# A gated linear recurrence on one Trainium2 core: both directions of a chunk share score products and one score matrix, and the backward state runs at the end

## The chip, the cores and the metric

The kernel runs on one core of one Trainium2 chip (trn2). The metric is the device time of one execution in microseconds (us). The engines are named as the profile names them: PE (matmuls), PEld (its weight loads), DVE, ACT, POOL and SP. SP and POOL issue most of the transfers here; their queues appear as SPq and POOLq.

## The reference, cut to what matters

One layer of a backbone: an input projection, two mixing branches (a 2-D Fourier transform over 2048 positions and the channels of four groups, and a gated linear recurrence run forwards and backwards), a merge, an output projection and an MLP. The change touches only the recurrence and the Fourier work that is interleaved with it. All of it is float32. Per direction and head (4 heads, 128 x 128 state):

```python
# S_t = diag(f_t) S_{t-1} + k_t v_t^T,   o_t = S_t^T q_t,   k = 1 - f
f = lb + (1.0 - lb) * sigmoid(f_pre)
scores = einsum('bhtk,bhsk,bhtsk->bhts', qc, kc, decay)   # inside a chunk, masked
o = o_inter(qc * exp(b), S) + einsum('bhts,bhsv->bhtv', scores, vc)
S_new = exp(b_last) * S + einsum('bhsk,bhsv->bhkv', kc * exp(b_last - b), vc)
o = o_f + o_b[:, :, ::-1]      # both directions are added
```

256 context tokens come first, and their final state starts the 2048 latent tokens, in each direction.

## The kernel before, in words

`phase_mix` (L600 to L1094) is one stage of the program. A **unit** is one chunk of 128 tokens in one direction: 4 context units, then 32 latent units, forward and backward alternating (`run`, L699). Forward units walk up from token 0, backward ones down from token 2047.

**Decays by levels.** The running products of the gates inside a chunk are built as a tree of 7 levels (block sizes B = 1 to 64, `LEVELS`). `gates` (L749) does per level two DVE multiplies of 128 x 512: the decayed operands for the score product (L755, `mix_lev`), then the tree step in place (L759, `mix_w`), which waits for L755. `mix_lev` holds for each position either its key or its query, by which half of its block of 2B it is in, so a product (L919) takes all 128 columns as weights and only the 64 query columns as the moving operand. There is one such product per level and head; a diagonal product with undecayed keys (L925) is separate. Every float32 matmul shows as two matmul instructions.

**Masking.** `mask_score` (L784) copies each score block under a mask into the unit's score matrix `pm` (L793, 128 x 256, six times; L798, 128 x 512, the diagonal); ACT copies level 64 (L1013). DVE interleaves the masking of unit k with the gates of unit k+1.

**State and output.** `whole` (L763) multiplies keys and queries by the whole-chunk decays (L769, 128 x 1024). PE transposes the keys (L856), ACT copies them (L959), PE forms the state's addition (L862), DVE makes the new state with four small instructions (L778). `output` (L896) takes 16 matmul instructions (L902, L903), ACT copies the result (L986) and POOL stores it (L1035).

**The rest of a unit.** In the first 16 latent units PE also does one Fourier unit of the first pass (two products of 128 x 512, L870), in the last 16 one of the second pass (L876 twice, L883). ACT makes keys 1 - f (L950), POOL writes ones (L1026). SP loads gates, queries and values of a unit once its predecessor's state is new (`slot`, L723: wait, then L732, L733, L734). All engines run hardware loops over 4 units (`Fori`).

Of the kernel before, what the change touches and what calls it, by code (L numbers as in the profile page):

```python
# [20 lines left out]
I32 = mybir.dt.int32  # L21
# [578 lines left out]
def phase_mix(nc, d, g):  # L600
# [3 lines left out]

    NU, NX, HP, W2 = 2 * NTT, TC // P, H * P, 2 * H * P
    SL = 4
    X = 2 * NX
    with Box(nc, "mix") as bx:
        w = bx.sb("w", [P, 2, 2, 2, HP])
        qk = bx.sb("qk", [P, 2, 2, 2, HP])
        v = bx.sb("v", [P, 2, 2, BR])  # L630
        lev = bx.sb("lev", [P, 2, NL, HP])
        qkd = bx.sb("qkd", [P, 2, 2, HP])
        pm = bx.sb("pm", [P, 2, HP])
        kdT = bx.sb("kdT", [P, 2, HP])
        st = bx.sb("st", [P, 2, HP])
        ost = bx.sb("ost", [P, 2, HP])
        mask = bx.sb("mask", [P, 2, NL - 1, 256], I32)
        diag = bx.sb("diag", [P, HP], I32)
        m1 = bx.sb("m1", [P, 2, 2, P])
        u_in = bx.sb("u_in", [P, 2, BR])  # L640
        a_st = bx.sb("a_st", [P, 2, 2, BR])
        m2 = bx.sb("m2", [P, 2, 2 * P])
        m3 = bx.sb("m3", [P, 2, P])
        xin = bx.sb("xin", [P, 2, 2, SL, P])
        zT = bx.sb("zT", [P, 2, 2, 512])
        fst = bx.sb("fst", [P, T])
        bank = bx.banks()
        SC, DG, TO, SS, FT = bank[0:4], bank[4], bank[5], bank[6], bank[7]
        ld_m = bx.sem("ld_m")
        ld = [[bx.sem(f"ld_{x}{s}") for s in range(2)] for x in "fb"]  # L650
        ld_n = [bx.sem(f"ld_n{i}") for i in range(2)]
        st_o, st_a = ([bx.sem(f"st_{n}{i}") for i in range(2)] for n in ("o", "a"))
        st_f = bx.sem("st_f")
        ld_x = [bx.sem(f"st_x{i}") for i in range(2)]
        step_s, ready, kk_done, ones, scores, masked, m64, trans, trcopy, o_mm, o_out, s_mm, s_new, f_mm, f_out = (
            bx.sem(n) for n in ("step", "lev_ready", "kk_done", "ones", "scores", "masked", "m64", "trans", "trcopy",
                                "o_mm", "o_out", "s_mm", "s_new", "f_mm", "f_out"))
        block = bx.block()
        ad = d["dft_a"]

        F2 = 2 * 16 - 12 * 4

        def at(i, k, per, c):

            return i * (SL * per) + (k * per + c)

        def halves(ap, B):
            return ap.rearrange("p (m two b) -> p m two b", two=2, b=B)  # L670

        def key_half(dr):
            return dr

        def halves_of(buf, dr, s, B):

            t = buf[:, dr, s]
# [18 lines left out]
        def pre_of(dr, s):  # L696
            return w[:, dr, s, 1 - key_half(dr)]
# [1181 lines left out]
```

## Time and profile before

| | us |
|---|---|
| median of 3 runs | 3809.98 (3809.21 to 3812.9) |
| span of the profiled execution | 3805.7 |
| what lies around that span, against the median | 4.3 |
| `phase_mix`, first load issued to last store issued | 1190.9 to 1757.4 |
| PE busy, share of the span | 3434.8 (90%) |
| DVE busy, share of the span | 1994.6 (52%) |

The profiled execution has no separate device time beside its span, so the span is compared with the median. The share of busy time is over the whole program; the stage that changes is one seventh of it and has its own limits. In the timeline an entry gives start, duration, engine, line, operation and count; a count above 1 merges neighbours, so the spacing of starts tells more than the durations, which overlap. PEclk is the granted TensorE clock: 1.00 is 2.4 GHz, 0.50 is 1.2 GHz.

### The profile page before, as it was taken

How to read it: one execution, taken by the hardware profiler on the slowest of the kernel's cores; microseconds unless marked ns; L12 is line 12 of the kernel's file. 1: busy time of each engine (PE TensorE's matmuls, PEld its weight loads, DVE VectorE, ACT ScalarE, POOL GpSimd, SP SyncE). 2: the span in 40 equal slices, each digit the busy share in tenths (PEclk: the TensorE clock that was granted, in tenths of full speed). 3: DMA queues.
4: the chain of work that ended last, by engine and by line, in shares of the span. 5: the costliest groups of instructions: out<-in, count | busy, mean ns of one | idle time of the engine just before them, and what ended most of it. 6: DMA issues, size and time to landing. Idle time of an engine off the chain costs nothing. (4 is left out here: it accounts for less than half of the span.)

```text
span 3805.7 us, 42879 instructions
## 1 busy us (share of the span) xinstructions
PE 3434.8 (90%) x16080; PEld 2863.9 (75%) x16080; DVE 1994.6 (52%) x2898; ACT 498.3 (13%) x825; POOL 211.1 (6%) x318
## 2 busy tenths in 40 slices
PE   6879999999896899996796968999999689999997
PEld 6867777777785788884575757888888478888885
DVE  3730000000124998995786658555555585555556
ACT  1211111111000122222100002111111021111110
POOL 0011100000000111110000000000000000000000
PEclk9699999999997788998898989999999899999998
DMA  6831122221213344342654342111111221111111
GB/s 209 279 119 66 66 66 77 72 66 56 77 64 104 102 124 123 111 122 105 194 168 151 134 161 72 44 44 44 50 44 50 86 86 58 47 44 44 49 50 45
DMA packets 257179, 349.40 MB, mean 92 GB/s; under 512 B 13107, under 2 KB 189507, under 8 KB 252358
## 3 DMA queue, kind: packets, MB, share of 16 engines
q1 hardware_dynamic: 225078, 221.86, 19.2%
q0 software_dynamic: 26208, 108.55, 8.2%
q10 hardware_dynamic: 5808, 17.83, 1.4%
q8 instruction: 56, 0.92, 0.1%
q14 instruction: 29, 0.24, 0.0%
HBM read 250.14 MB, written 98.05 MB: 91 GB/s over the span
## 5 line engine op out<-in xcount | busy, mean ns | idle before, releaser
L137 PE MATMUL mlp_bank<-mlp_h2h,mlp_w1h 128*128 128x512 f32 x1024 | 406.8, 397 | 23.0 <-ACT mlp_a L1670 23.0
L137 PE MATMUL proj_bank<-act_hTh,proj_wh 128*128 128x512 f32 x1024 | 401.8, 392 | 18.6 <-PE proj_bank L139 17.5
L1637 DVE TENSOR_TENSOR mlp_acc<-mlp_acc,mlp_bank 128x512 f32<-128x512 f32 x480 | 321.8, 685 | 175.6 <-PE mlp_bank L139 175.6
L137 PE MATMUL mlp_bank<-mlp_w2h,mlp_ah 128*128 128x512 f32 x1024 | 402.5, 393 | 9.8 <-DVE mlp_acc L1590 9.8
L139 PE MATMUL mlp_bank<-mlp_h2h,mlp_w1l 128*128 128x512 f32 x1024 | 406.0, 396 | 0.0
L138 PE MATMUL mlp_bank<-mlp_h2l,mlp_w1h 128*128 128x512 f32 x1024 | 405.9, 396 | 0.0
L139 PE MATMUL mlp_bank<-mlp_w2h,mlp_al 128*128 128x512 f32 x1024 | 401.1, 392 | 0.0
L138 PE MATMUL mlp_bank<-mlp_w2l,mlp_ah 128*128 128x512 f32 x1024 | 400.8, 391 | 0.0
L138 PE MATMUL proj_bank<-act_hTl,proj_wh 128*128 128x512 f32 x1024 | 398.6, 389 | 0.0
L139 PE MATMUL proj_bank<-act_hTh,proj_wl 128*128 128x512 f32 x1024 | 398.5, 389 | 0.0
L427 DVE CAST proj_wh<-proj_raw 128x1024 fp32r<-128x1024 f32 x40 | 27.8, 695 | 640.2 <-PEq L454 634.8
L919 PEld LDWEIGHTS mix_bank<-mix_lev 128*128 128x128 f32 x1792 | 238.7, 219 | 30.8 <-issue 22.6
L1628 DVE CAST mlp_ah<-mlp_a 128x512 fp32r<-128x512 f32 x128 | 54.9, 429 | 389.4 <-ACT mlp_a L1688 389.3
L919 PE MATMUL mix_bank<-mix_lev 128*128 128x64 f32 x1792 | 239.8, 302 | 21.1 <-DVE mix_pm L798 21.1
L137 PEld LDWEIGHTS mlp_bank<-mlp_h2h,mlp_w1h 128*128 128x128 f32 x1024 | 193.0, 189 | 70.4 <-ACT mlp_a L1670 23.5
L137 PEld LDWEIGHTS proj_bank<-act_hTh,proj_wh 128*128 128x128 f32 x1024 | 192.1, 188 | 70.6 <-issue 30.5
L1686 ACT ACTIVATE mlp_a<-mlp_bank,mlp_b 128x512 f32<-128x512 f32 x128 | 88.3, 689 | 1161.6 <-PE mlp_bank L139 1145.0
L137 PEld LDWEIGHTS mlp_bank<-mlp_w2h,mlp_ah 128*128 128x128 f32 x1024 | 193.6, 189 | 53.6 <-DVE mlp_acc L1590 13.3
L139 PEld LDWEIGHTS mlp_bank<-mlp_h2h,mlp_w1l 128*128 128x128 f32 x1024 | 192.9, 188 | 47.4
L138 PEld LDWEIGHTS mlp_bank<-mlp_h2l,mlp_w1h 128*128 128x128 f32 x1024 | 193.1, 189 | 47.0
L139 PEld LDWEIGHTS mlp_bank<-mlp_w2h,mlp_al 128*128 128x128 f32 x1024 | 193.7, 189 | 41.3
L138 PEld LDWEIGHTS mlp_bank<-mlp_w2l,mlp_ah 128*128 128x128 f32 x1024 | 193.7, 189 | 40.6
(204 smaller groups left out, 5204.2 us busy)
## 6 DMA issues: line engine op xcount, KB each, us to landing
mlp_raw<-in_w SPq DMA_DIRECT2D x128, 512.0 KB, 4.0
scratch_proj<-proj_stage POOLq DMA_DIRECT2D x32, 1024.0 KB, 5.3
front_w<-in_w_ada SPq DMA_DIRECT2D x24, 1024.0 KB, 5.6
proj_raw<-in_w_in SPq DMA_DIRECT2D x40, 512.0 KB, 5.8
merge_gates<-scratch_proj SPq DMA_DIRECT2D x32, 512.0 KB, 5.1
front_x<-in_x ACTq DMA_DIRECT2D x8, 1024.0 KB, 6.1
scratch_xn<-front_x POOLq DMA_DIRECT2D x8, 1024.0 KB, 6.4
mix_w<-scratch_proj SPq DMA_DIRECT2D x32, 256.0 KB, 3.1
```

The source lines that it names most:

```text
L137: nc.tensor.matmul(out, wh, xh, start=(k == 0), stop=False)
L138: nc.tensor.matmul(out, wh, xl, start=False, stop=False)
L139: last = nc.tensor.matmul(out, wl, xh, start=False, stop=(k == k_tiles - 1))
L427: nc.vector.tensor_copy(wh[:, s], raw[:, s]).then_inc(w_hi, 1)
L919: last = nc.tensor.matmul(SC[li // 2][:, (li % 2) * 256 + h * 64:(li % 2) * 256 + h * 64 + 64], lv, halves(lv, B)[:, :, 1 - key_half(dr)], ...
L1628: nc.vector.tensor_copy(ah[:, z, cs], a[:, c, :]).then_inc(ahi_s, 1)
L1637: nc.vector.tensor_tensor(dst, dst, V[n % 4][:], ALU.add).then_inc(acc_s, 1)
L1686: nc.scalar.activation(a[:, c, :], U[2 * e + c][:], ACT.Relu, bias=bias).then_inc(relu_s, 1)
```

## The change

The stage is rewritten. A **chunk** now holds both directions: 2 context chunks, then 16 latent ones, walked forwards, all unrolled.

1. DVE per level: one multiply of 128 x 1024 makes keys and queries for both directions (`level`), and two tree steps of 128 x 512 (`tree`). The operand `kq` is a ring of 5 levels, and `level` waits for its own completion.
2. PE per level: one product of 128 x 128 per head fills the score blocks of both directions. Level 64 is made of two 64-wide products per head. The diagonal product takes the sum of both directions' keys, which POOL adds (`key_sum`).
3. One score matrix per chunk: six masked copies of 128 x 512 on DVE, levels 32 and 64 by six small ACT copies (`big`).
4. The forward output of a chunk already holds the scores of both directions. The backward state needs the chunks from the last to the first, so the decayed backward queries (`qd`), the additions (`ub`) and the totals (`tot`) of all chunks are kept, and after the last chunk 16 steps of `back_state`, `back_output` and a store follow.
5. Fourier units: 8 of the first pass ahead of everything, 2 a chunk in chunks 0 to 3, one of the second pass a chunk in chunks 4 to 15, the last 4 in the tail. Fourier products have two banks (`FT`).
6. A chunk needs 5 loads: two gates, the queries twice, the values.

The diff, cut to its core (of the removed lines only the loops stand here; the functions that they called are printed above):

```diff
-            for k in range(SL):
-                slot(0, k, 1)
-            with eng.Fori(1, 4) as i:
...
         @block.sync
+            def load_f(n):
+                b = n % 2
+                if n >= 2:
+                    sp.wait_ge(kd_s, n - 1)
+                    sp.wait_ge(tot_s, n - 1)
...
+                for row, dr in ((3, 0), (1, 1)):
+                    sp.dma_start(dec[:, b, row].rearrange("p (h t) -> p h t", h=H),
+                                 src[dr * BR:(dr + 1) * BR, cols].rearrange("(h p) t -> p h t", p=P)).then_inc(ld_f[b], 16)
+            def load_q(n):
+                b, c = n % 2, n - NX
+                if c >= 2:
+                    sp.wait_ge(qd_s, c - 1)
+                    sp.wait_ge(sc_s, 8 * (c - 2) + 1)
+                for row in (1, 3):
...
+            def load_u(j):
+                if j >= 2:
+                    sp.wait_ge(f_mm, 2 * (j - 2) + 2)
...
+            for n in range(NX):
+                load_f(n)
+                load_v(n)
+            sp.dma_start(mask[:], d["masks"]).then_inc(ld_m, 16)
+            load_q(NX)
+            for j in range(2):
+                load_u(j)
...
+            for j in range(2, 8):
+                load_u(j)
+            load_f(NX)
+            load_f(NX + 1)
+            for c in range(NC):
...
+                if c + 1 < NC:
+                    load_v(n + 1)
+                if c + 2 < NC:
+                    load_q(n + 2)
+                    load_f(n + 2)
         @block.vector
+            def tree(n, li):
+                B = LEVELS[li]
+                out, total = forward(n % 2, B)
+                step.up(nc.vector.tensor_tensor(out, out, total, ALU.mult))
+                out, total = backward(n % 2, B)
+                step.up(nc.vector.tensor_tensor(out, out, total, ALU.mult))
+            def level(c, li):
...
+                nc.vector.tensor_tensor(kq[:, r % NK, :], selected(qk[:, b].rearrange("p a t -> p (a t)"), LEVELS[li]),
+                                        selected(decays(b), LEVELS[li]), ALU.mult).then_inc(lev_s, 1)
+                dve.wait_ge(lev_s, r + 1)
...
+            def new_state(n):
+                dve.wait_ge(u_mm, 2 * n + 1)
...
+            for c in range(NC):
+                n = c + NX
+                loaded(n)
+                dve.wait_ge(ld_q[n % 2], 32 * ((c // 2) + 1))
+                for li in range(NL):
+                    level(c, li)
+                    tree(n, li)
+                    if li == 1:
+                        new_state(n - 1)
+                    if li == 2 and c == 0:
+                        dve.wait_ge(ub_s, 2)
+                        back_state(0, ub[:, NC - 1], tot[:, 0, 1], ub[:, NC - 2])
+                    if li < 6:
+                        score(c, li)
+                    step.wait(dve)
+                keys(n)
+                queries(c)
+            new_state(NU - 1)
+            for x in range(1, NC):
+                c = NC - x
+                if x >= 2:
+                    dve.wait_ge(o_mm, NC + x - 1)
+                dve.wait_ge(ub_s, NX + c + 1)
+                back_state(x, sb_[:, (x + 1) % 2], tot[:, NX + c, 1], ub[:, c])
         @block.tensor
+            for j in range(8):
+                for piece in range(2):
+                    fourier("a", j, piece)
+            transposes(0, 0)
+            transposes(0, 1)
...
+                diagonal(c)
+                level(c, 0)
+                transposes(n - 1, 0)
+                fourier(*parts[0])
+                level(c, 1)
+                transposes(n - 1, 1)
+                products(n - 1, 0)
+                level(c, 2)
+                fourier(*parts[1])
+                products(n - 1, 1)
+                level(c, 3)
+                if c:
+                    output(c - 1)
+                level(c, 4)
+                fourier(*parts[2])
+                level(c, 5)
+                if len(parts) > 3:
+                    fourier(*parts[3])
+                level(c, 6)
...
+            for x in range(NC):
+                back_output(x)
+                if x < len(rest):
+                    fourier("b", *rest[x])
         @block.scalar
...
+                key_copy(n - 1, 0)
+                fourier(*parts[0])
+                key_copy(n - 1, 1)
+                fourier(*parts[1])
+                back_copy(n - 1)
+                if c:
+                    output(c - 1)
+                fourier(*parts[2])
+                if len(parts) > 3:
+                    fourier(*parts[3])
+                big(c)
+                totals(n)
+                if c + 2 < NC:
+                    keys(n + 2)
...
         @block.gpsimd
+            def key_sum(c):
+                n = c + NX
+                pool.wait_ge(kk, n + 1)
...
+                nc.gpsimd.tensor_tensor(ks[:, c % 2], qk[:, n % 2, 0], qk[:, n % 2, 2], ALU.add).then_inc(ksum, 1)
```

In the last excerpt `keys` on ACT waits for both gate loads of its chunk, makes the two sets of keys and counts `kk`; `totals` copies the last decay columns once DVE has counted `kd_s` in `keys`; `products` on PE waits for the ACT copy of the transposed keys.

## Rows read from the trace of the kernel before

**Rows 1.** The page: span and instructions.

```profile
span 3805.7 us, 42879 instructions
```

**Rows 2.** Busy time by stretch: stretch, length, PE, PEld, DVE, ACT, POOL (count), PEclk, DMA, GB/s.

```profile
1242.00:1500.00 258.00, 233.84 (x1493) 208.55 (x1492) 236.33 (x413) 52.44 (x95) 40.65 (x67) 0.82 0.41 120
1500.00:1740.00 240.00, 235.23 (x1658) 210.29 (x1657) 219.66 (x387) 57.90 (x134) 40.48 (x60) 0.99 0.35 106
```

**Rows 3.** Timeline of DVE: one unit, and the first and last L769 of the loop.

```profile
1236.16 1.23 DVE L769 TENSOR_TENSOR mix_qkd<-mix_qk,mix_w 128x1024 f32<-128x1024 f32 x1
...
1577.81 1.22 DVE L769 TENSOR_TENSOR mix_qkd<-mix_qk,mix_w 128x1024 f32<-128x1024 f32 x1
1579.03 0.84 DVE L755 TENSOR_TENSOR mix_lev<-mix_qk,mix_w 128x512 f32<-128x512 f32 x1
1579.91 1.11 DVE L759 TENSOR_TENSOR mix_w<-mix_w 128x512 f32<-128x512 f32 x1
1581.05 0.69 DVE L755 TENSOR_TENSOR mix_lev<-mix_qk,mix_w 128x512 f32<-128x512 f32 x1
...
1589.27 0.68 DVE L759 TENSOR_TENSOR mix_w<-mix_w 128x512 f32<-128x512 f32 x1
1589.87 0.73 DVE L798 COPY_PREDICATED mix_pm<-mix_diag,mix_bank 128x512 f32<-128x512 int32 x1
1590.49 0.68 DVE L755 TENSOR_TENSOR mix_lev<-mix_qk,mix_w 128x512 f32<-128x512 f32 x1
...
1592.03 1.12 DVE L778 SCALAR_TENSOR_TENSOR mix_st<-mix_st,mix_w,mix_bank 128x128 f32<-128x128 f32 x4
...
1737.30 1.22 DVE L769 TENSOR_TENSOR mix_qkd<-mix_qk,mix_w 128x1024 f32<-128x1024 f32 x1
```

**Rows 4.** Timeline of PE: the first two at clock 0.50, the others at 1.00.

```profile
1240.31 1.91 PE L870 MATMUL mix_bank<-mix_u_in,mix_m 128*128 128x512 f32 x2
...
1261.93 2.02 PE L925 MATMUL mix_bank<-mix_qk 128*128 128x128 f32 x8
...
1737.70 6.36 PE L919 MATMUL mix_bank<-mix_lev 128*128 128x64 f32 x56
...
1743.90 1.11 PE L925 MATMUL mix_bank<-mix_qk 128*128 128x128 f32 x8
...
1744.85 1.89 PE L876 MATMUL mix_bank<-mix_m,mix_xin 128*128 128x256 f32 x8
```

**Rows 5.** Busy time by stretch where the clock falls and comes back.

```profile
1315.00:1316.00 1.00, 0.22 (x2) 0.23 (x3) 1.00 (x3) 0.32 (x2) 1.00 (x2) 1.00 0.82 249
1318.00:1331.00 13.00, 13.00 (x55) 11.63 (x55) 12.83 (x22) 0.74 (x2) 0.00 (x0) 0.50 0.21 62
1331.00:1332.00 1.00, 1.00 (x4) 0.41 (x4) 0.96 (x2) 0.44 (x1) 0.00 (x0) 0.89 0.00 0
```

**Rows 6.** Timeline of SP: a unit's first two load issues.

```profile
1561.36 0.37 SPq L732 DMA_DIRECT2D mix_w<-scratch_proj  x1
...
1561.91 0.40 SPq L733 DMA_DIRECT2D mix_qk<-scratch_proj  x1
```

**Rows 7.** Issue to landing of the third load (L734), 1240 to 1490 us.

```profile
DMA to landing us min/median/max: 3.3/3.8/6.4
```

**Rows 8.** Timeline of ACT: two sets of keys, one copy of a bank.

```profile
1224.63 1.34 ACT L950 ACTIVATE mix_qk<-mix_w,all_one 128x512 f32<-128x512 f32 x2
...
1755.75 0.59 ACT L986 COPY mix_ost<-mix_bank 128x512 f32<-128x512 f32 x1 [1.20 <-PE mix_bank L903]
```

**Rows 9.** Busy time by stretch, columns as in Rows 2: the stage's first loads.

```profile
1190.00:1200.00 10.00, 0.00 (x0) 0.00 (x0) 5.22 (x7) 0.72 (x1) 3.40 (x7) 0.50 0.71 148
1200.00:1210.00 10.00, 4.30 (x16) 3.21 (x16) 9.66 (x17) 2.69 (x5) 0.17 (x1) 0.50 0.74 285
```

**Rows 10.** Transfers of the stage, size and median us to landing.

```profile
scratch_o<-mix_ost POOLq DMA_DIRECT2D x30, 256.0 KB, 3.2
```

**Rows 11.** Timeline of POOL: the stage's last store.

```profile
1756.63 0.75 POOL L1035 DMA_DIRECT2D scratch_o<-mix_ost  x1 [1.23 <-ACT mix_ost L986]
```

More of the change, by code:

```diff
@@ L653, in phase_mix @@
+        st_o, st_a, ld_x = ([bx.sem(f"st_{x}{s}") for s in range(2)] for x in "oax")
         st_f = bx.sem("st_f")
[L654 to L657, printed above, removed]
+        step_s, kk, ones, ksum, lev_s, sc_s, masked, big_s, kd_s, qd_s, tot_s = (bx.sem(x) for x in (
+            "step", "keys", "ones", "key_sum", "level", "scores", "masked", "big", "keys_decayed", "queries_decayed", "totals"))
@@ L658, in phase_mix @@
+        trans, trcopy, u_mm, ub_s, new_s, o_mm, o_out, b_new, f_mm, f_out = (bx.sem(x) for x in (
+            "trans", "trcopy", "u_mm", "u_back", "state", "o_mm", "o_out", "state_back", "f_mm", "f_out"))
         block = bx.block()
         ad = d["dft_a"]
[L663 to L673, printed above, removed]
@@ new lines, in back_output @@
+            def back_output(x):
+                c = NC - 1 - x
+                pe.wait_ge(b_new, x + 1)
+                pe.wait_ge(o_out, NC + x)
+                for h in range(H):
+                    s = slice(h * P, (h + 1) * P)
+                    last = nc.tensor.matmul(OUT[:, s], sb_[:, x % 2, s], qd[:, c, s], start=True, stop=True)
+                last.then_inc(o_mm, 1)
+            for j in range(8):
+                for piece in range(2):
+                    fourier("a", j, piece)
@@ L947, in _ @@
+            transposes(NU - 1, 0)
+            transposes(NU - 1, 1)
+            fourier("b", 12, 0)
+            products(NU - 1, 0)
+            output(NC - 1)
+            fourier("b", 12, 1)
+            products(NU - 1, 1)
+            rest = [(j, piece) for j in range(12, 16) for piece in range(3)][2:]
+            for x in range(NC):
+                back_output(x)
+                if x < len(rest):
+                    fourier("b", *rest[x])
         @block.scalar
         def _(act):
-            def one_minus_f(dr, s):
-                nc.scalar.activation(qk[:, dr, s, key_half(dr)], pre_of(dr, s), ACT.Identity, scale=-1.0, bias=g["one"][:, 0:1]
-                                     ).then_inc(kk_done, 1)
@@ L1023, in _ @@
+            key_copy(NU - 1, 0)
+            key_copy(NU - 1, 1)
+            fourier("b", 12, 0)
+            output(NC - 1)
+            fourier("b", 12, 1)
+            back_copy(NU - 1)
+            rest = [(j, piece) for j in range(12, 16) for piece in range(3)][2:]
+            for x in range(NC):
+                output(NC + x)
+                if x < len(rest):
+                    fourier("b", *rest[x])
         @block.gpsimd
         def _(pool):
-            def suf_ones(dr, s):
-                nc.gpsimd.memset(w[:, dr, s, key_half(dr)], 1.0).then_inc(ones, 1)
```

708 lines of the change are left out of this document (345 added, 363 removed).

## The prediction, written before the changed kernel ran

> **What bounds the kernel now.** I read the page first: one execution spans 3805.7 us [rows 1], and only `phase_mix`, 1190.9 to 1757.4, is changed. Next the stretches of that stage: with the first-pass Fourier units PE is busy for 233.8 of 258 us and DVE for 236.3, at a mean granted clock of 0.82; with the second pass PE for 235.2 of 240 and DVE for 219.7, at 0.99 [rows 2]. Both engines are nearly full, so a cut on one alone buys only its lead over the other. Then DVE's timeline: from the first to the last L769 of the loop it is 501.1 us for 31 units, 16.2 us each [rows 3]; a unit on DVE, summed below by the same prices, is 15.1 us, so the remaining 1.1 us is DVE waiting for PE.
>
> **DVE, a chunk of both directions** [rows 3]. Spacing of starts counts, not duration. A multiply of 128 x 512 takes 0.60 us when the next instruction does not wait for it (1589.27 to 1589.87), its 0.69 plus 0.035 when it does; at B = 1 it takes 0.84 (L755) or 1.11 (L759). A multiply of 128 x 1024 takes 1.22. A masked copy of 128 x 512 takes 0.62 (1589.87 to 1590.49), the state 1.12. Hence:
> - levels 1 to 5: 1.255 (`level`, waited for) + 2 x 0.60 (`tree`) + 0.62 (`score`) = 3.08 each, 15.4;
> - level 0: 1.55 (1.255 plus twice the 0.15 that B = 1 adds to 0.69) + 2 x 1.02 + 0.62 = 4.2;
> - level 6, without a score: 1.255 + 0.60 + 0.725 = 2.6;
> - new state 1.12, keys 1.13, queries 1.22: 3.5.
>
> Sum 25.7 us a chunk, against 32.3 us measured for two units. That alone would give 16 x 6.6 = 106 us. Most of it goes again, at three places.
>
> **PE, a chunk.** At full clock 56 products of 64 columns take 6.36 us, 0.114 each, and 8 of 128 columns take 1.11 with their end, 0.111 from start to start [rows 4]. A 64-column product costs what a 128-column one does, so a level for both directions costs what one direction did: 0.9 us. Diagonal 0.9, six levels 5.4, level 64 (16 short products) 0.9 to 1.8, two sets of transposes (4 instructions each, half the group) 1.2, two of products 1.8, output 1.8, Fourier 3.4 (first pass, the low-clock 1.91 of L870 halved, four times) or 5.1 (L876 twice, and L883 like it): 16 to 17.5 us of 25.7. PE is no longer the bound at full clock; at half clock it needs 32 to 35.
>
> **First loss: a chain through four queues, every chunk.** Let E be the end of `queries`. SP waits for it, then issues four loads (queries twice, gates twice) about 0.5 apart [rows 6]; before, the first went out 0.17 after the state. The third load of a unit, issued 1.1 after the first, lands 3.8 later, 3.3 at the least [rows 7]; the fourth I put 0.9 behind it (an estimate: the issue distance of 0.55 and a little more transfer), so the gates are there at E + 5.85. ACT has `keys(n+2)` ahead of the `key_copy` of the next chunk: 1.34 for two sets, 0.59 for the copy [rows 8], done at E + 7.9. Only then can PE run the second set of transposes and the products (0.6 + 1.05): E + 9.65. DVE reaches `new_state`, which needs them, after level 0, level 1 and its tree: E + 4.2 + 2.46 = E + 6.7. It waits 3.0 us at full clock. At half clock these PE steps double: 4.3, and 5.8 if the level and the second-pass Fourier product ahead of them are at half clock too. By the least landing and full clock it is 2.4. In the last chunk, which follows no such loads, PE's order alone costs 1.4. I take 3.6, near the full-clock end because PE has wide products here: a chunk of 29.3 us, bounds 28.1 and 31.5. Behind the waiting `new_state` stand all further levels; PE idles for 3 us there, so nothing catches up.
>
> **Second loss: the head.** The first load goes out at 1190.9, and ahead of the first Fourier input stand 2.8 MB. By 1200 the queues had moved 1.5 MB, in the next 10 us 2.9 MB [rows 9]: it is there at about 1204. Eight Fourier units follow on PE before any key is transposed. Each must store two halves before its buffer is free: a store of that size lands after 3.2 [rows 10], plus copies and two issues 5.4 us for two units, so 2.7 each, to 1227. DVE's context work, 2 x 11.4 us, ends by 1220 and hides there. The gates of chunk 0 wait on SP for `totals(0)`, which is on ACT behind the eight units; loads, keys: DVE starts chunk 0 at 1233. It waits there for its two states (4 to 8 us, the first ones at low clock) and adds one `back_state`: chunk 0 takes 33, to 1266.
>
> **Third loss: the tail.** After the last chunk PE does transposes, two Fourier pieces, products and one output: the first `back_output` starts 9.5 us later (8.2 at full clock). Ten steps are a `back_output` of 0.9 and a Fourier piece of 1.73: 26.3. The last six are bound by the copy and store loop, 0.59 + 3.2 and hand-overs for two steps, 2 us, or 2.7 at low clock: 15.7 with the last store. 51.5 in all, bounds 50 and 56; before, the loop's last L769 was followed by 19 us to the end of the last store [rows 3, 11].
>
> **The sum.** 1266 + 14 x 29.3 + 27.5 (last chunk) + 51.5 = 1755.2, against 1757.4: 2 us shorter, a span of 3803.5. The median of the runs stands 4.3 above the span, so 3808 us. What follows the stage is unchanged. What the hardware loops cost per pass before is inside the 16.2; the unrolled chunks have no such term.
>
> **POOL's addition** (`key_sum`, 128 x 512) has no row; the nearest is POOL busy for 40.65 us with 67 entries [rows 2], 0.6 each. It starts when the keys are made, E + 7.3, while DVE waits for PE anyway. Beside DVE work it can cost nothing or hold DVE up for its own length; I take nothing, because it falls into the wait.
>
> **The clock.** After about 1.4 us in which PE had nothing to do (busy for 0.22 of the us from 1315, and for a part of the one before it) it ran from 1318 to 1331 at 0.50, the 1.2 GHz level, though busy all the time and mostly with 64-column products, and came back to 2.4 GHz in 1331 to 1332, behind 128- and 512-column ones [rows 5]. The new chunk leaves PE without work for about 3 us at two places, ahead of level 0 and behind `new_state`'s products, so stretches at half clock follow; I expect a mean of 0.65 to 0.8 in this stage, and have put 0.6 us for it into the wait of 3.6.
>
> **Rivals.**
> - *The chain is short.* The loads land like the fastest ones, PE is at full clock when the key copies come: 28.1 a chunk, 17 us less, and the head and tail at their short ends, another 5: 3786. For it: the least landing of 3.3, and no other queue is transferring at E. Against it: four loads instead of three. With the wait at its floor of 1.4, which only an order without the keys ahead of the copy would allow, 3772.
> - *Half clock decides.* Place: level 0, the Fourier piece and the transposes ahead of `new_state`. PE comes into each chunk after 3 us without work, so at 0.50: a wait of 5.8, 31.5 a chunk, +31, and 5 more in chunk 0 and the tail: 3844. It ends slower from a chunk of 30.0 on. For it: 0.82 already where PE was busy 9 tenths of the time [rows 2]. Against it: these products are twice as wide as those that ran for 13 us at 0.50 [rows 4, 5].
> - *POOL and DVE block each other.* If the chain is short, `key_sum` no longer falls into DVE's wait but beside its multiplies; with 0.6 us lost in each of 14 chunks on top of the forecast, 3816. It weighs most against the short chain. The Trainium skill, SBUF — State Buffer (section Who interferes with whom) has the rule for it: a DVE instruction with two SBUF inputs and a GpSimd instruction that reads SBUF contend, and the loser stands still. Before, POOL only wrote (its memsets), so no row bears on it; chance 0.03.
> - *The diff does not do what it says.* If each direction still had its own masked copies and its own products, DVE would stay at 16 us a direction; the diff speaks against it; 0.02.
>
> **The numbers.** A measurement of this kernel can tell 0.2%, 7.6 us, from no change. My forecast (waits near 3.6) has 0.36, the short chain 0.31, half clock 0.28, POOL 0.03, the diff 0.02. An error of 0.5 us in a chunk is already 8 us, so the middle case keeps 0.30 within 0.2%, and its rest is split between the sides: faster 0.36, slower 0.34. The forecast's own range is 3797 to 3819. Both large rivals belong in 8 of 10, short of the outermost floor: 3776 to 3847.
>
> **What would show it.** DVE without waits 25.7 a chunk; `new_state` waiting for PE's products 3 to 4.5 us in chunks 1 to 14 and 1.4 in the last; ACT's keys starting near E + 6; DVE's first `level` at 1233; 16 backward steps in about 41 us; PE busy for about 75% of the stage. Wrong would be: DVE waiting at the scores (PE late all over), a unit price of 128 x 1024 above 1.22, or a head that is much shorter because the Fourier units are not bound by their stores.

## The result, and the profile of the changed kernel

The median is 3817.62 us in 14 runs (3811.38 to 3825.12), beside 3809.60 for the kernel before in 14 runs on the same chip: a ratio of 1.0023, 95% interval [1.0015, 1.0031]. The change makes the kernel slower by 8 us (5.7 to 11.8). I had forecast 3808, a gain of 2: the time is inside the range of 3776 to 3847, but it moved the other way.

The profiled execution took 3825.12 us, the longest of the 14 and 7.5 above their median. The page and the busy time by stretch (columns as in [rows 2]); the recurrence runs from 1198.6 to 1778.6:

```profile
span 3823.4 us, 39338 instructions
PE 3322.9 (87%) x15056; PEld 2737.5 (72%) x15056; DVE 1936.6 (51%) x2650; ACT 532.7 (14%) x943; POOL 228.8 (6%) x313
```

```profile
1198.60:1244.00 45.40, 22.49 (x56) 9.80 (x56) 22.91 (x35) 14.74 (x28) 11.58 (x20) 0.76 0.83 254
1244.00:1377.00 133.00, 83.11 (x473) 65.44 (x474) 105.55 (x138) 32.01 (x74) 22.33 (x30) 0.82 0.32 98
1377.00:1700.00 323.00, 225.13 (x1452) 193.28 (x1452) 276.29 (x363) 82.70 (x209) 52.03 (x60) 0.89 0.27 82
1700.00:1740.00 40.00, 32.95 (x201) 28.75 (x202) 27.84 (x45) 11.10 (x27) 5.28 (x8) 0.87 0.17 56
1740.00:1778.60 38.60, 32.39 (x172) 26.67 (x171) 14.82 (x52) 14.43 (x30) 13.85 (x19) 0.87 0.41 126
```

What to see: the stage lasts 580.0 us against 566.4 before (1190.9 to 1757.4), +13.6. What stands ahead of it is the same code and took 7.7 us longer in this execution; in the twelve kernels below it took 1188.7 to 1197.3, so that is scatter. What follows took 3.5 less. So the span moved by 17.7 and the median by only 8; differences of a stage to these 580.0 can come out some us too large. PE was busy for 91 and 98% of the stretches of [rows 2]; now it has work for 62% of the second stretch and 70% of the third. DVE, at 79 to 86%, no longer fills its time either: neither engine's own work sets the length, so a wait between them does.

The chain of waits between engines names it. Columns: engine, its line, whom it waited for; us in total, times, the longest:

```profile
ACT mix_qk L1001 <- DMA mix_dec<-scratch_proj: 108.3, 16, 9.7
...
DVE mix_st L792 <- PE mix_bank L891: 72.6, 17, 7.2
...
PE mix_bank L858 <- DMA mix_fx<-in_dft_m: 38.6, 9, 19.3
...
DVE mix_kd L763 <- PE mix_bank L878: 14.0, 1, 14.0
```

The second line is the wait of `new_state` that the forecast is built on. It isn't the same in all chunks. From one L769 to the next, chunks 1 to 5 take 32.75, 32.01, 32.71, 32.11 and 31.83 us with waits of 7.24, 6.51, 7.20, 6.61 and 6.33; chunks 6 to 14 take 28.4 to 29.5 (28.9 on average) with 2.9 to 4.0; chunk 15 takes 27.62 with 2.11. Here is a late chunk (chunk 2) on the timeline (columns: start, us, engine, line, operation, count, idle time before and what ended it):

```profile
1311.67 0.99 SPq L687 DMA_DIRECT2D mix_dec<-scratch_proj  x2
1312.70 0.50 SPq L710 DMA_DIRECT2D mix_fx<-scratch_u  x1
1314.20 0.44 SPq L711 DMA_DIRECT2D mix_fx<-in_dft_m  x1
...
1317.68 0.72 ACT L1001 ACTIVATE mix_qk<-mix_dec,all_one 128x512 f32<-128x512 f32 x1 [7.88 <-DMA mix_dec<-scratch_proj]
1318.84 2.04 PE L858 MATMUL mix_bank<-mix_fx 128*128 128x512 f32 x2 [3.88 <-DMA mix_fx<-in_dft_m]
...
1322.07 0.60 PE L878 MATMUL mix_bank<-all_ident,mix_kd 128*128 128x128 f32 x4
1322.51 1.06 PE L891 MATMUL mix_bank<-mix_v,mix_kdT 128*128 128x128 f32 x8
1323.60 1.12 DVE L792 SCALAR_TENSOR_TENSOR mix_st<-mix_st,mix_tot,mix_bank 128x128 f32<-128x128 f32 x4 [6.51 <-PE mix_bank L891]
```

SP issues its loads in the order of the program. Its four loads for the chunk after next wait for L769 (end 1310.60 here), and **behind them stand the Fourier inputs of the chunk that has just begun**, issued from 1312.70 on. PE has a Fourier piece ahead of level 1, of the second transposes and of the products that the state needs. So it stands still for 3.88 us until the input has landed, and DVE behind it. And a steady chunk (11, the longest of the nine), with E, the end of L769, at 1582.71:

```profile
1583.76 1.00 SPq L687 DMA_DIRECT2D mix_dec<-scratch_proj  x2
...
1586.51 2.61 PE L864 MATMUL mix_bank<-mix_m,mix_fx 128*128 128x256 f32 x8
...
1589.60 0.72 ACT L1001 ACTIVATE mix_qk<-mix_dec,all_one 128x512 f32<-128x512 f32 x1 [7.69 <-DMA mix_dec<-scratch_proj]
1590.96 0.59 ACT L1015 COPY mix_kdT<-mix_bank 128x512 f32<-128x512 f32 x1
1591.60 0.66 PE L878 MATMUL mix_bank<-all_ident,mix_kd 128*128 128x128 f32 x4 [1.58 <-ACT mix_kdT L1015]
1592.09 1.06 PE L891 MATMUL mix_bank<-mix_v,mix_kdT 128*128 128x128 f32 x8
1593.19 1.12 DVE L792 SCALAR_TENSOR_TENSOR mix_st<-mix_st,mix_tot,mix_bank 128x128 f32<-128x128 f32 x4 [4.00 <-PE mix_bank L891]
```

That is the forecast's chain link by link: gates issued, landed, ACT's keys, the key copy behind them, transposes, products. It holds in all nine steady chunks: ACT's keys start 5.8 to 6.9 us after E (6.2 on average), and the wait is that time less 2.9 in eight of them, less 2.7 in chunk 12. The head and the tail:

```profile
1237.40 0.30 ACT L1008 COPY mix_tot<-mix_dec 128x4 f32<-128x4 f32 x2
...
1239.01 1.23 DVE L763 TENSOR_TENSOR mix_kd<-mix_qk,mix_dec 128x1024 f32<-128x1024 f32 x1 [13.98 <-PE mix_bank L878]
...
1242.28 0.72 ACT L1001 ACTIVATE mix_qk<-mix_dec,all_one 128x512 f32<-128x512 f32 x1 [2.75 <-DMA mix_dec<-scratch_proj]
...
1243.69 1.26 POOL L1110 TENSOR_TENSOR mix_ks<-mix_qk 128x512 f32<-128x512 f32 x1 [3.86 <-ACT mix_qk L1002]
1243.91 2.43 DVE L755 TENSOR_TENSOR mix_kq<-mix_qk,mix_dec 128x1024 f32<-128x1024 f32 x1 [2.88 <-ACT mix_qk L1002]
...
1738.92 1.05 PE L948 MATMUL mix_bank<-mix_qd,mix_stb 128*128 128x128 f32 x8
1741.54 1.05 PE L948 MATMUL mix_bank<-mix_qd,mix_stb 128*128 128x128 f32 x8
...
1771.56 2.05 PE L948 MATMUL mix_bank<-mix_qd,mix_stb 128*128 128x128 f32 x8 [0.77 <-ACT mix_ost L1034]
1774.37 2.05 PE L948 MATMUL mix_bank<-mix_qd,mix_stb 128*128 128x128 f32 x8 [0.77 <-ACT mix_ost L1034]
```

DVE's second set of context keys waits 14 us for transposes that PE does behind all eight Fourier units. The first chunk's multiply (L755) comes 45.3 us after the stage's start; it waits another 2.88 us for ACT's keys, whose gates SP issues at 1237.79, behind the totals that ACT copies at 1237.40, after its sixteen Fourier copies. In the tail a backward step with a Fourier piece takes 2.62; without one 1.9, and 2.8 at the low clock.

### The profile page after: what moved, and what is told of

Same layout as the page of the kernel before. It is cut to its first block and busy times, and to the rows that moved or that the text cites. A ratio compares the mean times of both kernels' runs of the same rounds, so it can differ in the third digit from the quotient of the medians.

```text
span 3823.4 us, 39338 instructions
## 1 busy us (share of the span) xinstructions
PE 3322.9 (87%) x15056; PEld 2737.5 (72%) x15056; DVE 1936.6 (51%) x2650; ACT 532.7 (14%) x943; POOL 228.8 (6%) x313
## 5 line engine op out<-in xcount | busy, mean ns | idle before, releaser
L427 DVE CAST proj_wh<-proj_raw 128x1024 fp32r<-128x1024 f32 x40 | 27.8, 695 | 640.3 <-PEq L454 635.0
L139 PEld LDWEIGHTS proj_bank<-act_hTh,proj_wl 128*128 128x128 f32 x1024 | 192.2, 188 | 40.2
L138 PEld LDWEIGHTS proj_bank<-act_hTl,proj_wh 128*128 128x128 f32 x1024 | 192.3, 188 | 38.8
```

Of the source, the lines that this page charges most:

```text
L138: nc.tensor.matmul(out, wh, xl, start=False, stop=False)
L139: last = nc.tensor.matmul(out, wl, xh, start=False, stop=(k == k_tiles - 1))
L427: nc.vector.tensor_copy(wh[:, s], raw[:, s]).then_inc(w_hi, 1)
```

## The experiments

Each kernel was run beside the kernel before. "Stage" is the length of the recurrence in the profiled execution (566.4 before, 580.0 after); the ratio is to the kernel before, with its 95% interval. The kernels stand in the order of the questions. The ratio is not the quotient of the two medians, so the two columns can differ by a few us; most in e3, whose ten times lie in two groups, four at 3796 to 3802 and six at 3814 to 3818 (the profiled one among them).

| kernel | ratio | median, difference to before | stage |
|---|---|---|---|
| e1_u_first | 1.0010 [0.9998, 1.0022] | +5 | 570.2 |
| e2_gates_first | 1.0006 [0.9994, 1.0018] | +3 | 564.1 |
| e3_keys_behind | 1.0004 [0.9987, 1.0021] | +9 | 576.6 |
| e5_sum_beside_mult | 1.0058 [1.0041, 1.0075] | +21 | 584.1 |
| e4_u_and_gates | 0.9966 [0.9956, 0.9977] | -15 | 550.5 |
| e6_ug_sum_at_state | 0.9968 [0.9956, 0.9980] | -13 | 552.9 |
| e7_head | 1.0040 [1.0025, 1.0055] | +19 | 581.5 |
| e8_all | 0.9961 [0.9947, 0.9976] | -13 | 552.6 |
| e9_piece_behind | 1.0050 [1.0031, 1.0069] | +16 | 577.7 |
| e10_keys_between | 0.9969 [0.9958, 0.9981] | -13 | 552.9 |
| e11_piece_too | 0.9965 [0.9951, 0.9978] | -14 | 538.2 |
| e12_version | 0.9951 [0.9936, 0.9967] | -22 | 542.5 |

**1. Is it SP's order? (e1)** The Fourier inputs go out ahead of the loads that wait for L769.

```diff
             load_f(NX + 1)
+            for j in range(8, 10):
+                load_u(j)
             for c in range(NC):
                 n = c + NX
-                for j in range(8 + 2 * c, 10 + 2 * c):
-                    if j < 16:
-                        load_u(j)
                 if c + 1 < NC:
                     load_v(n + 1)
+                for j in range(10 + 2 * c, 12 + 2 * c):
+                    if j < 16:
+                        load_u(j)
```

> Change against the changed kernel: SP issues the Fourier inputs of chunk c+1 (load_u) ahead of its wait for the queries of chunk c, not behind the four loads that follow that wait. Queue theory (in chunks 1 to 3 the wait of new_state is 6.3 to 7.2 us instead of 3 because PE's Fourier piece stands in front of the transposes and its input is issued behind four other loads): the wait falls to 3 to 4 us in chunks 1 to 3, PE's idle time ahead of L858 (38.6 us for its transfers in all) loses 8 to 12 us, and the kernel gets 9 to 12 us faster, to about 3807. Clock theory (these chunks are slow because PE is at 0.50 there): the wait stays above 5.5 us and the time stays within 3 us of 3817.

Chunks 1 to 3 now take 28.87, 29.40 and 30.26 us with waits of 3.38, 3.93 and 4.77; chunk 4 stays late (33.71, 32.11 in the changed kernel). The stage is 9.8 us shorter, 8.9 of it in these three chunks. Chunk 2:

```profile
1308.82 1.19 PE L860 MATMUL mix_bank<-mix_fx 128*128 128x512 f32 x2
...
1311.50 0.72 ACT L1003 ACTIVATE mix_qk<-mix_dec,all_one 128x512 f32<-128x512 f32 x1 [7.63 <-DMA mix_dec<-scratch_proj]
...
1315.09 1.12 DVE L794 SCALAR_TENSOR_TENSOR mix_st<-mix_st,mix_tot,mix_bank 128x128 f32<-128x128 f32 x4 [3.93 <-PE mix_bank L893]
```

With E at 1304.68, PE's Fourier piece starts 4.1 us after it instead of 8.2, and the gates are last again, as in a steady chunk. By the profiles SP's order is the cause of 8.9 of the 14.9 us that the forecast missed in chunks 1 to 5. By the ratios (1.0010 against the changed kernel's 1.0023) the edit is worth about 5 us, not the 9 to 12 that I expected, and the two intervals touch.

Chunk 4 has another cause: POOL issues the first loads of the second pass there, and PE's first piece of it waits for them (in the changed kernel 2.85 us, up to 1382.53; here 4.97, up to 1372.36). In the changed kernel the gates are late in it too: ACT's keys start 8.9 after E, which less 2.9 makes 6.0 of the wait of 6.6. Chunk 5 has no Fourier input from SP in its way: its keys start 8.0 after E, and its transposes and products ran at the low clock (1.12 and 1.92 us instead of 0.60 and 1.06), so its wait is the keys' time less 1.65. It took 28.49 in e1 and 30.76 in e7; why its gates land late, no run shows.

**2. Is the chain of the gates what sets a steady chunk? (e2, e3)** The first loads the gates ahead of the queries; the second takes ACT's keys from ahead of the key copies to behind both.

```diff
-                    load_q(n + 2)
                     load_f(n + 2)
+                    load_q(n + 2)
```

> Change against the changed kernel: of the four loads behind the end of a chunk the two gates go out first, the queries behind them. Chain theory (new_state waits for gates, ACT's keys, ACT's key copy, PE's transposes and products): in chunks 6 to 14 the gates are there 1.7 us earlier, the wait of new_state falls from 3.0 to 4.0 us to 1.4 to 2.2, a chunk from 28.9 to about 27.2, and the kernel gets 14 to 22 us faster. Rival, PE's order alone sets the wait (level 1, the Fourier piece and low clock ahead of the transposes): less than 5 us. If POOL's addition, which then runs beside DVE multiplies, blocks them, each chunk gives back up to 1.2 us of it and a DVE multiply of 0.69 or 1.22 us shows a duration longer by about that much.

Chunks 6 to 14 take 27.4 to 27.7 (one 29.0) with waits of about 1.1 instead of 2.9 to 4.0; chunks 1 to 4 stay at 31.4 to 33.2, as they should if it is the Fourier inputs, on SP or POOL, that make them late. The waits fell by 2.2, the chunks by 1.1 (28.9 to 27.8). The rest went here:

```profile
1599.66 1.20 DVE L755 TENSOR_TENSOR mix_kq<-mix_qk,mix_dec 128x1024 f32<-128x1024 f32 x1
1600.88 1.27 POOL L1110 TENSOR_TENSOR mix_ks<-mix_qk 128x512 f32<-128x512 f32 x1 [5.30 <-ACT mix_qk L1002]
1600.89 1.80 DVE L745 TENSOR_TENSOR mix_dec<-mix_dec 128x512 f32<-128x512 f32 x1
```

POOL's key sum now falls beside a multiply, and the multiply takes 1.80 instead of 0.69. The stage is 15.9 us shorter, but the ratio (1.0006) gives only about 6 us against the changed kernel, where I had expected 14 to 22.

```diff
                 totals(n)
-                if c + 2 < NC:
-                    keys(n + 2)
...
                 key_copy(n - 1, 1)
+                if 1 <= c < NC - 1:
+                    keys(n + 1)
                 fourier(*parts[1])
```

> Change against the changed kernel: ACT makes the keys of the next-but-one chunk behind the two key copies, not ahead of them; the loads keep their order. Chain theory: the key copy no longer waits for any load, the wait of new_state falls to PE's order alone, 1.4 us (to 2.5 at low clock) in chunks 6 to 15, and the kernel gets 18 to 28 us faster; in chunks 1 to 3 it falls only if the Fourier input is not what PE waits for, so by the queue theory it stays near 6 there. Rival: nothing, if PE is held by something else.

Steady chunks of 28.0 with waits of 2.1 to 2.2, every third 29.3 with 3.47; chunks 1 to 3 stay late. The stage is only 3.4 us shorter and the ratio (1.0004) gives about 7 us; I had expected 18 to 28, since I took the wait to fall to 1.4. Both edits shorten the same chain at another link, and the steady chunks follow in both, so the chain is shown. After either of them something else is last, at 1.1 and 2.2: questions 4 and 5.

**3. Do POOL and DVE block each other? (e5)** The key sum is held until the state is there, so that it runs beside the next multiplies.

```diff
                     suffix_ones(n + 2)
+                    pool.wait_ge(new_s, n + 1)
                     key_sum(c + 2)
```

> Change against the changed kernel: POOL's key_sum (128 x 512, two inputs in SBUF, 1.27 us) waits for the new state of the next chunk, so it runs beside DVE's multiplies of level 2 instead of in DVE's wait. Port theory (a DVE multiply with two SBUF inputs and POOL's read hold each other up for the whole length): one multiply in each of 14 chunks shows 1.0 to 1.3 us more, and the kernel gets 14 to 18 us slower. Rival, both run beside each other: DVE's durations stay at 0.69 and 1.22 and the time stays within 3 us of 3817.

```profile
1561.75 0.74 DVE L780 COPY_PREDICATED mix_pm<-mix_mask,mix_bank 128x512 f32<-128x512 int32 x1
1561.80 1.26 POOL L1110 TENSOR_TENSOR mix_ks<-mix_qk 128x512 f32<-128x512 f32 x1 [11.19 <-DVE mix_st L792]
1562.38 1.77 DVE L755 TENSOR_TENSOR mix_kq<-mix_qk,mix_dec 128x1024 f32<-128x1024 f32 x1
```

The stage grows by 4.1 us, 0.55 in each steady chunk (the ratio, 1.0058, by about 13 us): the multiply takes 1.77 instead of 1.21, half of the 1.0 to 1.3 that I had expected. The masked copy that ran beside the key sum at first keeps its 0.74. The key sum ended at 1563.06, 0.68 after the multiply had begun, so a multiply is held about as long as the two overlap. In e2 they began together and it lost 1.1; in the head of the changed kernel it is 2.43 instead of 1.45. The Trainium skill, SBUF — State Buffer (section Who interferes with whom) says that a DVE instruction with two SBUF inputs contends with a GpSimd instruction that reads SBUF, and one with at most one SBUF input, outside the 2-port modes, does not; these rows agree.

**4. Both loads forward, and the key sum out of the way (e4, e6).** e4 is e1 and e2 together; e6 also holds the key sum until the state's products are done, beside instructions that it doesn't hold up.

```diff
                     suffix_ones(n + 2)
+                    pool.wait_ge(u_mm, 2 * n + 1)
                     key_sum(c + 2)
```

> Both loads put forward at once: the Fourier input ahead of the four loads that wait for the queries' multiply, and in those four the gates ahead of the queries. Queue theory and chain theory together (the two waits are independent): chunks 1 to 3 as in the first edit, 29 us at most, and with the gates early 27.7; chunks 6 to 14 27.7; chunk 4 stays late by the two Fourier loads on POOL (32 to 33). Stage about 580.0 - 9.8 (first edit alone) - 15.9 (second alone) = 554 to 557 us, ratio to before .997 to .998. Rival (one cover, two wants: the early gates bring the Fourier input of the next chunk no nearer, or the two edits shorten the same wait): stage near the better of the two alone, 564. The port theory wants a multiply of about 1.75 beside each key sum here too, and therefore 27.7 and not 26.6 as the steady chunk.

> As the last kernel (both loads put forward) and the key sum on POOL held until the first decayed products of the chunk are there, so that it runs beside the state's four instructions and a masked copy, none of which was lengthened by it so far. Port theory (a VectorE multiply with both inputs in SBUF and the key sum on POOL exclude each other, other instructions do not): no multiply over .75 (512 wide) or 1.25 (1024 wide) in a steady chunk, chunks 6 to 14 of 26.6 to 26.9, stage 8 to 10 us shorter than with the loads put forward alone (about 546). Rival (the key sum costs VectorE 1.1 us wherever it runs, or the diagonal product that waits for it becomes late): chunks of 27.7 as before the edit.

e4: chunks 1 to 3 of 27.75, 26.76 and 27.79, steady chunks of 27.7, a stage of 550.5 where the two gains alone give 554.3. The two waits are independent, and this version beats both kernels by the ratio too (0.9966). e6: no multiply is lengthened any more, and nothing is won: steady chunks of 27.67, waits of 2.2. I was wrong there. In e4 the held multiply stood ahead of the wait and only shortened it (1.76 for L749 at 1584.49, and a wait of 0.87 behind it); what sets the chunk is on PE, as the next two kernels show.

**5. What is last then? (e10, e11)** On top of e6, ACT's keys move between the two key copies (e10); then also PE's Fourier piece behind the first decayed products, and its copy behind the second key copy (e11).

```diff
                 transposes(n - 1, 0)
-                fourier(*parts[0])
                 level(c, 1)
                 transposes(n - 1, 1)
                 products(n - 1, 0)
+                fourier(*parts[0])
                 level(c, 2)
```

> The key-sum kernel (both loads put forward, key sum beside the state) with ScalarE's two key operations moved between the two key copies. Chain theory (in the key-sum kernel 2.2 us of wait are left because the first key copy waits on ScalarE behind the keys, 1613.75 to 1615.1, while its transposes were done at 1613.6): the wait falls by 1.3 to 1.5 us to about .8, steady chunks 26.2 to 26.6, stage 552.9 - 15 x 1.2 = 535. Rival (TensorE's first Fourier piece at the low clock, 2.9 us, is last once the copies are early): the wait falls by under .6 us, chunks of 27.1 and up, stage over 545.

> The kernel before in this list plus the Fourier piece behind the first decayed products. If the keys-between kernel's rival is right (the piece is last), this takes its wait away: steady chunks at VectorE's own 25.6 to 26.2 us, and chunk 4 loses its extra wait (33.3 to about 27), stage 525 to 532. If the copies are what is last, only chunk 4 gains: 6 us less than the keys-between kernel.

e10 changes nothing: 27.67, 2.19. Its timeline says why:

```profile
1582.37 3.22 PE L866 MATMUL mix_bank<-mix_m,mix_fx 128*128 128x256 f32 x8
1582.61 0.59 ACT L1017 COPY mix_kdT<-mix_bank 128x512 f32<-128x512 f32 x1 [4.25 <-PE mix_bank L880]
...
1586.32 0.60 PE L880 MATMUL mix_bank<-all_ident,mix_kd 128*128 128x128 f32 x4
1586.76 1.06 PE L893 MATMUL mix_bank<-mix_v,mix_kdT 128*128 128x128 f32 x8
1587.85 1.12 DVE L794 SCALAR_TENSOR_TENSOR mix_st<-mix_st,mix_tot,mix_bank 128x128 f32<-128x128 f32 x4 [2.19 <-PE mix_bank L893]
```

The first key copy ended at 1583.2, but the Fourier piece takes 3.22 us at the lower clock (1.89 at the full one, [rows 4]), and level 1 and the transposes stand behind it. e11 takes it out: chunks of 26.74 with a wait of 1.25, chunk 4 among them (32.94 before), and a stage of 538.2, 14.7 less than e10. I had expected chunks of 25.6 to 26.2 and a stage of 525 to 532. Every third chunk still takes 28.5, with products at the low clock:

```profile
1550.24 1.12 DVE L794 SCALAR_TENSOR_TENSOR mix_st<-mix_st,mix_tot,mix_bank 128x128 f32<-128x128 f32 x4 [1.25 <-PE mix_bank L893]
...
1577.18 1.47 PE L893 MATMUL mix_bank<-mix_v,mix_kdT 128*128 128x128 f32 x8
...
1578.69 1.12 DVE L794 SCALAR_TENSOR_TENSOR mix_st<-mix_st,mix_tot,mix_bank 128x128 f32<-128x128 f32 x4 [2.96 <-PE mix_bank L893]
```

The medians don't follow the stage here: e11's is 14 us under before, as e10's, and its profiled execution (3781.2) was its second fastest of ten (3779.9 to 3800.9). I take 26.74 as what a chunk can do, not what it does in most runs.

**6. The same move on the changed kernel (e9).** Only the Fourier piece and its copy move.

> On the changed kernel, one move: the first Fourier piece of a chunk stands behind the first decayed products on TensorE, and its copy behind the second key copy on ScalarE. Queue theory (the Fourier input that SP issues late reaches the state only because a Fourier piece stands ahead of the products): the waits for the state fall in chunks 1 to 3 from 6.5 to 7.2 us down to what the steady chunks have, 3 to 4, chunk 4 from 6.6 to about 4, so stage 12 to 16 us shorter (564 to 568); chunks 6 to 14 keep 28.4 to 29.5, since there the copy of the keys is last (-.5 at most). Rival (the early chunks are late because their gates land late beside 128 KB of other loads, whatever the order on TensorE): chunks 1 to 3 of 32 us, stage 578 to 580.

Both theories were off. Chunks 1 to 3 lose what set them apart, with waits of 4.88, 4.77 and 4.64 instead of 6.5 to 7.2; that agrees with SP's order as the cause. But the steady chunks go from 28.9 to 30.0, so the stage is only 2.3 us shorter in the profile, and by the ratio (1.0050 against 1.0023) the kernel is slower than the changed one:

```profile
1581.72 0.59 ACT L1015 COPY mix_kdT<-mix_bank 128x512 f32<-128x512 f32 x1
1582.36 1.11 PE L878 MATMUL mix_bank<-all_ident,mix_kd 128*128 128x128 f32 x4 [0.70 <-ACT mix_kdT L1015]
1583.27 1.91 PE L891 MATMUL mix_bank<-mix_v,mix_kdT 128*128 128x128 f32 x8
1585.22 1.12 DVE L792 SCALAR_TENSOR_TENSOR mix_st<-mix_st,mix_tot,mix_bank 128x128 f32<-128x128 f32 x4 [4.36 <-PE mix_bank L891]
```

With the gates late, the Fourier piece ahead cost no time and did something useful: PE was at 2.4 GHz when the transposes and products came (0.60 and 1.06). Without it they run at 1.2 GHz (1.11 and 1.91); the mean granted clock between 1410 and 1660 us is 0.84 against 0.89. The keys start 6.2 after E on average in both kernels, but the wait is now that time less 1.6 (less 2.3 in chunk 8) instead of less 2.9: the clock alone is the difference. In the profiles the same move wins 14.7 us of stage where the chain is short (6.2 of them in chunk 4) and loses 1.1 us a chunk where it is long.

**7. The head (e7, e8, e12).** In e7 context chunk 0's transposes and its first products stand behind two Fourier units instead of eight (its second ones behind six), the gates of the first chunk are loaded behind the fifth Fourier load, and its key sum stands after six stores.

```diff
             for j in range(8):
                 for piece in range(2):
                     fourier("a", j, piece)
-            transposes(0, 0)
-            transposes(0, 1)
-            products(0, 0)
-            products(0, 1)
+                if j == 1:
+                    transposes(0, 0)
+                    transposes(0, 1)
+                    products(0, 0)
+                if j == 5:
+                    products(0, 1)
```

> On the changed kernel, the head alone: the transposes and the first decayed products of context chunk 0 stand behind two of the eight Fourier units instead of behind all eight on TensorE and ScalarE, the first chunk's gates are loaded behind the fifth Fourier load, and its key sum stands after six of the stores. If the 14 us wait of the second keys' multiply is what delays the first chunk, that wait falls under 1 us and the first chunk's first multiply comes at +35 to +41 us from the stage's start instead of +45.3, limited then by the Fourier pieces that stand ahead of its diagonal product; the stage is 4 to 10 us shorter (570 to 576). Rival (the first chunk waits for its gates' landing and for the Fourier units in any case): +45, stage 580 within 1.5 us.

The 14 us wait is gone, and the first chunk's multiply comes at +39.8 instead of +45.3. The chunk then ends at +81.9 instead of +79.3, because `new_state` in it waits 9.32 us, and the stage of 581.5 misses the 570 to 576 that I had expected:

```profile
1239.08 1.01 SPq L687 DMA_DIRECT2D mix_dec<-scratch_proj  x2
...
1241.92 0.44 SPq L711 DMA_DIRECT2D mix_fx<-in_dft_m  x1
...
1246.42 2.04 PE L859 MATMUL mix_bank<-mix_fx 128*128 128x512 f32 x2 [6.63 <-DMA mix_fx<-in_dft_m]
...
1251.57 0.61 DVE L793 SCALAR_TENSOR_TENSOR mix_st<-mix_st,mix_tot,mix_bank 128x128 f32<-128x128 f32 x2 [9.32 <-PE mix_bank L892]
```

It is SP's order once more: the first chunk's Fourier input stands behind the gates of the second, and these wait for totals that ACT takes behind all sixteen Fourier copies. e8 put e6, this head and a second bank for the tail together:

> All of it together, as a version: both loads put forward, key sum beside the state's instructions, the head's order of the last kernel, and in the tail the backward outputs alternate between two banks of the accumulator (OUT and the transposes' bank). Terms: stage 546 from the key-sum kernel, less 4 to 10 of the head, less 6 steps x .8 = 4.8 of the tail's last steps (with one bank a step without a Fourier piece takes 1.9 = products 1.05 + copy .59 and handoffs; with two it is bounded by the products, about 1.1) = 531 to 537 us; ratio to before .990 to .992. Should the head's gain be taken back by the first chunk, 537 to 541.

With 552.6 it is no better than e6 and far from the 531 to 541 expected, the head's gain being paid back in chunk 0 (a wait of 9.12) as in e7. e12 is e11 with this head, both totals behind the sixth unit, and backward outputs that alternate between two PSUM banks:

> All of it as a version: both loads put forward, keys between the key copies, key sum beside the state, the Fourier piece behind the first products, in the head context chunk 0's transposes and products behind two Fourier units and both chunks' totals behind six, and two banks in the tail. Against the piece-too kernel: first multiply 5 us earlier, and no longer paid back, since the Fourier pieces that waited for their input stand behind the products; tail 2 us shorter. Stage 518 to 527 us, ratio to before .987 to .990. If the head's gain is paid back again, 525 to 530.

The stage of 542.5 misses the expected 518 to 530. e12's first multiply comes at +37.6 and its first chunk ends at +71.1 (+78.8 in e11), so the head is worth 7.7 us once nothing takes it back. In the profiled execution three chunks of four take 28.3 to 28.9, at a mean clock of 0.85 between 1410 and 1660 us (e11: 0.89), which costs more than the head gave. By the medians it is the fastest kernel here, 21.7 us under before, though its interval overlaps e11's. The tail is 49.0 against e11's 49.7; I had expected 2 less. With one bank e2, e5 and e7 have 49.2, so no gain of the second bank is shown.

## Why the prediction was right or wrong

Against the forecast's own terms, for the profiled execution (7.5 us above the median of the runs, so the differences add up to more than the 9.6 by which the median missed):

| term | forecast | measured | difference |
|---|---|---|---|
| stage start to chunk 0 | 42.1 | 45.3 | +3.2 |
| chunk 0 | 33 | 34.0 | +1.0 |
| chunks 1 to 5 | 5 x 29.3 | 161.4 | +14.9 |
| chunks 6 to 14 | 9 x 29.3 | 260.0 | -3.7 |
| chunk 15 | 27.5 | 27.6 | +0.1 |
| tail | 51.5 | 51.8 | +0.3 |
| sum | 564.3 | 580.0 | +15.7 |

**The step that failed** is "14 x 29.3": the wait was worked out once and taken for all of them. I wrote that SP waits for L769 and then issues four loads, but didn't ask what is queued behind them on SP. It is the Fourier input of the chunk under way, and only up to chunk 3, where the first pass ends; and PE's piece that needs it stands ahead of the state's products. In chunks 1 to 3 the term is 3.2 us a chunk against the 29.3; e1 takes 3.0 of it away, and e9 shows it from the other side. Chunks 4 and 5 add 2.8 and 2.5. A direct reading would have found it: of all orders behind a wait, which does another engine need first?

**Chunk 4** has the same shape on POOL's queue, the first loads of the second pass, and late gates beside it. Kernels with the Fourier piece behind the products lose it (e11, 26.76; e12, 28.33; in part e9, 31.48); those with the piece ahead keep it (32 to 35).

**Right was** the price list of DVE: a chunk less its wait is 25.5 (28.54 less 3.04, and the same in e11, 26.74 less 1.25), against 25.7. Right was the steady chain with its links: keys at E + 6.2 on average (forecast 5.85) and the wait 2.9 less than that (2.85 by my terms). That the wait came to 3.3 where I had taken 3.6 is in part luck: the landing was 0.4 us longer, and the 0.6 that I had put in for the clock was hardly needed there. Right was the tail: first `back_output` 9.4 after E (9.5), ten steps in 26.7 (26.3), the rest 15.6 (15.7). Chunk 15 is luck: 27.5 is 0.4 more than the forecast's own 25.7 + 1.4, and the wait was 2.1.

**The head** was 3.2 too short, in two halves: the Fourier units ended 37.9 after the start of the stage and not 36.1, though ACT's copies do wait for the stores as I had written, and from there to the first multiply it took 7.5 and not 6 (totals, gates, ACT's keys). That DVE's second context keys wait for transposes behind those units I had missed too, but that wait ends at 1239.01, and the first multiply waits for ACT's keys up to 1243.91: it isn't what delayed the chunk.

**The clock** was 0.76 to 0.89 by stretch, not 0.65 to 0.8, and PE had work for 68% of the stage (396 of 580 us), not 75. The rival "half clock decides" fell: none of chunks 6 to 14 reached 30. Its mechanism is real, though: it adds 1.3 us to the wait of chunk 5, and it sets e9's products and e10's Fourier piece. My 4.3 for the doubled steps doesn't follow from its own terms (3.0 + 1.65); e9's steps, 2.86 from the first transpose to the state against 1.59, bear out the 4.3.

**POOL's addition** at nothing was right for the changed kernel's steady chunks, since it fell into the wait. As a rival it was undersized: up to 1.1 us and not 0.6, since the addition takes 1.26.

**Where the gain of 106 us went** (16 chunks of 6.6): 66 into the waits of `new_state` in chunks 1 to 15 (33.9 in chunks 1 to 5, 30.1 in 6 to 14, 2.1 in the last) and 8 into chunk 0, 34.0 where 25.7 are work. That leaves 32 to 34 in the chunks. The tail takes 33 of them back (51.8 where [rows 3, 11] give 19), and the head 15 more: DVE starts 45.3 us into the stage, and before it had the first unit's L769 done at 46.4, so it began that unit at about 30. Together that is the 14 us of loss in the profiled execution; the medians show 8. e11's stage is 42 us shorter with the same arithmetic, by order alone, though its ratio of 0.9965 gives only about 22 us against the changed kernel. Not settled is why the medians of e11 and e10 agree while their stages differ by 14.7, nor why those of e1 to e3 move less than I expected; single executions were profiled, and no run here shows the others' clocks in this stage.

## What to carry to other kernels

Where a queue's order waits for something late in an iteration, list what stands behind it and who needs that first, separately for the iterations whose lists differ; a term that is multiplied by 14 must be checked in the first, the middle and the last. Ahead of a state that is carried on, put only what the state needs, but look at what that does to TensorE's clock: a piece that waits for nothing can be worth its place if the chain behind it is late anyway, and costs its full low-clock length if it isn't. And put a GpSimd operation that reads SBUF beside copies and PSUM-fed instructions, not beside two-input multiplies; here (e6) that alone won nothing, since PE was last.

## What the runs showed of the hardware that I had not expected

- A POOL addition of 128 x 512 takes 1.26 us, and a DVE multiply with both inputs in SBUF is held for about as long as the two overlap (0.69 to 1.80, 1.21 to 1.77, 1.45 to 2.43). The masked copy (0.72 to 0.74) and the state's instructions (1.12) beside it were not. POOL can be held too: in e4 an addition took 1.66 where multiplies ran.
- The low clock came and went by a rhythm over several chunks, with identical code in each: in e11 every third chunk was 1.7 us longer, in e12 three of four were 1.6 to 2.2 us longer.
- In chunks 6 to 14 the two loads of gates took 4.8 to 5.8 us (5.2 on average) from the first issue to the start of ACT's keys when they followed two loads of queries, and 3.6 to 4.4 (3.9) in e4, where they were the first of the four.
- The wait at the end of the chain showed the clock more sharply than its mean did: keys' start less 2.9 us where the transposes and products ran at 2.4 GHz, less 1.6 where they ran at 1.2.
